# The expert stage of a mixture-of-experts encoder layer in 32-token blocks: plain f32 products on 32-column tiles, three experts' weights on chip

## What is computed

```python
e_idx, gw = route(uf, w_router, router_bias)   # best of 8 groups, then best 2 of its 4 experts
...
def expert_block(args):                        # xblk: tokens of one expert
    xblk, e = args
    h = jax.nn.silu(xblk @ w_gate[e]) * (xblk @ w_up[e])   # 1024 -> 512, twice
    return h @ w_down[e]                                   # 512 -> 1024
...
y = segment_sum(yb * buf_w[:, None], buf_tok, num_segments=N)
```

## Time and profile before

| | |
|---|---|
| runs (median, range) | 2013.12 us (2011.57 to 2013.32), 3 runs |
| profiled execution | 2008.88 us, of which the traced span is 2007.0 us |
| expert stage in the trace | 1233.7 us (first transposes) to 1948.7 us (last write issued) |
| after it | 58.3 us to the end of the span |
| PE busy over the span | 87% |

### The profile page before, as it was taken

The page is one execution under the profiler, slowest core; times in us unless marked ns, Lnnn a source line. Parts: engine busy times, 40 slices in busy tenths (PEclk is TensorE's granted clock), DMA queues, the critical chain, the costliest instruction groups (busy, mean ns, idle before and its releaser), DMA issues.

```text
span 2007.0 us, 24786 instructions
## 1 busy us (share of the span) xinstructions
PE 1742.4 (87%) x8132; PEld 1397.1 (70%) x8133; DVE 1128.1 (56%) x1313; ACT 863.5 (43%) x1011; POOL 457.7 (23%) x303
## 2 busy tenths in 40 slices
PE   3899999999776999999989923999999999999970
PEld 1767787776545787787868822877777777777760
DVE  1534343445766334343236671466888878878538
ACT  1423333334653111101022120467887887878623
POOL 3411122211123333233312123111221212212112
PEclk7989999999887999999999956999999999999995
DMA  8101111101502333341222143476999999999626
GB/s 287 42 22 42 31 41 31 41 11 28 195 0 84 112 113 100 99 152 47 89 95 97 42 180 106 188 303 261 380 393 376 382 387 375 388 384 376 280 101 234
DMA packets 124566, 346.03 MB, mean 172 GB/s; under 512 B 17758, under 2 KB 79846, under 8 KB 112238
## 3 DMA queue, kind: packets, MB, share of 16 engines
q1 hardware_dynamic: 99678, 272.55, 36.4%
q0 software_dynamic: 10800, 36.77, 5.3%
q10 hardware_dynamic: 14048, 36.20, 5.1%
HBM read 309.21 MB, written 36.29 MB: 172 GB/s over the span
## 4 chain that ended last, share of the span: by engine, by line
PE 67%; DVE 14%; DMA 6%; ACT 4%; issue 2%; POOL 1%; ACTq 0%; DVEq 0%; POOLq 0%; SPq 0%
PE ps L678 22%; PE ps L904 8%; PE ps L905 7%; PE ps L909 7%; PE ps L838 5%; PE ps L863 4%; DMA raw_u<-in_w_exp_up 3%; PE ps L754 3%; PE ps L720 3%; DMA ada_g<-in_ada_w 1%; PE ps L745 1%; PE ps L804 1%; DVE wg_lo L354 1%; DVE wu_lo L354 1%; DMA raw_g<-in_w_exp_gate 1%
## 5 line engine op out<-in xcount | busy, mean ns | idle before, releaser
L678 PE MATMUL ps<-u_hi,w_hi 128*128 128x512 f32 x768 | 315.2, 410 | 16.9 <-POOL w_lo L514 16.3
L678 PE MATMUL ps<-u_hi,w_lo 128*128 128x512 f32 x768 | 302.9, 394 | 0.0
L678 PE MATMUL ps<-u_lo,w_hi 128*128 128x512 f32 x768 | 302.7, 394 | 0.0
L678 PEld LDWEIGHTS ps<-u_hi,w_hi 128*128 128x128 f32 x768 | 146.3, 190 | 50.2 <-issue 24.4
L513 POOL CAST w_hi<-w_raw 128x1024 fp32r<-128x1024 f32 x48 | 53.0, 1104 | 538.5 <-PE ps L678 453.7
L678 PEld LDWEIGHTS ps<-u_hi,w_lo 128*128 128x128 f32 x768 | 145.6, 190 | 31.9
L678 PEld LDWEIGHTS ps<-u_lo,w_hi 128*128 128x128 f32 x768 | 146.7, 191 | 25.7
L354 DVE TENSOR_TENSOR wd_lo<-raw_d,wd_hi 128x2048 fp32r<-128x2048 f32 x64 | 143.8, 2288 | 23.7 <-ACT wd_hi L350 23.7
L616 POOL COPY tok_cur<-tokl 128x1 int32 x37 | 26.8, 723 | 545.4 <-PE ps L893 545.4
L1088 ACT ACTIVATE gate<-ps,bg 128x512 f32<-128x512 f32 x48 | 33.0, 689 | 270.3 <-PE ps L678 229.4
L354 DVE TENSOR_TENSOR wu_lo<-raw_u,wu_hi 128x2048 fp32r<-128x2048 f32 x64 | 143.4, 2280 | 0.0
(11 more groups left out here) (277 smaller groups left out, 3598.0 us busy)
## 6 DMA issues: line engine op xcount, KB each, us to landing
raw_g<-in_w_exp_gate SPq DMA_DIRECT2D x32, 2048.0 KB, 9.4
raw_u<-in_w_exp_up SPq DMA_DIRECT2D x32, 2048.0 KB, 10.4
raw_d<-in_w_exp_down SPq DMA_DIRECT2D x32, 2048.0 KB
d_y<-yb ACTq DMA_DIRECT2D x37, 512.0 KB, 9.7
ada_g<-in_ada_w ACTq DMA_DIRECT2D x32, 512.0 KB, 3.8
w_raw<-in_w_in SPq DMA_DIRECT2D x24, 512.0 KB, 4.1
w_raw<-in_w_branch_gate SPq DMA_DIRECT2D x24, 512.0 KB, 4.1
ada<-in_ada_w SPq DMA_DIRECT2D x4, 2048.0 KB, 15.1
```

The source lines that it names most:

```text
L678: ins = pe.matmul(ps[:, 5 + h, :], a[par][:, kc, :], b[:, kc, HF[h]], start=(n == 1), stop=(n == MM))
```

## The change

The expert stage is rewritten. Blocks have 32 tokens. A block's 32 rows of 1024 are gathered as 128 pieces of 1 KB, so that all 128 partitions are used. The products are plain f32, without a split: gate and up together are 8 steps of four matmuls (32 stationary columns, 256 moving columns, one for each quarter of the output), down is 4 steps of four. The raw weights are used as they land, in three slots (`w_exp`, 48 KB per partition each); slot reuse waits for the last block of the expert three back (`gu_ps`, `y_ps`). Experts come in the order 0, 4, 8, ..., 28, 1, 5, ..., since `group_at` is the identity. ACT, DVE and POOL have one loop over all blocks; PE's experts are unrolled. In each turn PE transposes the hidden rows of block j-1 and the gathered rows of block j+1, does gate and up of block j, and down of block j-1 (numbered from 1; the first turn's down is of nothing, so there are 94 writes).

```diff
-CAP = 128
-NBLK = 2048 // CAP + NE
+CAP = 32
+LEAST = 2
+NBLK = 2048 // CAP + LEAST * NE
+SLOTS = 3
+QT = D // 4
...
+def group_at(g):
+    return g
+def expert_at(i):
+    return EPG * group_at(i % NG) + i // NG
...
+            for i in range(SLOTS, NE):
+                used = sp.value_load(starts[0:1, i - 2:i - 1], min_val=LEAST + 1, max_val=NBLK + 1)
+                sp.wait_ge(gu_ps, used)
+                for w in "gu":
+                    load_expert(i, w)
+                sp.wait_ge(y_ps, used)
+                load_expert(i, "d")
...
-                pool.wait_ge(xg_ps, j + 1)
+            with pool.Fori(1, end) as j:
+                pool.wait_ge(ld_xg, j * 16)
                 hold(pool)
                 pool.tensor_copy(tok_cur[:], tokl[:, bass.ds(j + 1, 1)]).then_inc(tok_ready, 1)
-                pool.wait_ge(tok_ready, j + 2)
+                pool.wait_ge(tok_ready, j + 1)
+                pool.wait_ge(xg_ps, j)
                 hold(pool)
+                gather_rows()
...
+            def gate_up(sl):
+                for kc in range(KC):
+                    x = xT[:, kc % 2, CAP * (kc // 2):CAP * (kc // 2 + 1)]
+                    for n in range(4):
+                        off = part_of["gu"[n // 2]] + kc * FE + QT * (n % 2)
+                        last = pe.matmul(ps[CAP * n:CAP * (n + 1), 2, 0:QT], x, w_exp[:, sl, off:off + QT],
+                                         start=(kc == 0), stop=(kc == KC - 1))
+                last.then_inc(gu_ps, 1)
...
+            def turn(j, sl, d_slot):
+                hidden_turn(j)
+                pe.wait_ge(xT_ready, j)
+                pe.wait_ge(ld_xg, j * 16 + 16)
+                hold(pe)
+                rows_to_features()
+                gate_up(sl)
+                down_turn(j, d_slot)
...
             def output(j):
-                sc.wait_ge(y_ps, j + 1)
-                sc.wait_ge(st_y, j * 16 + 16)
-                sc.activation(yb[:], ps[:, 5:7, :].rearrange("p a b -> p (a b)"), ACT.Copy).then_inc(y_evac, 1)
+                sc.wait_ge(y_ps, j)
+                sc.wait_ge(st_y, j * 16)
+                sc.activation(yb[:], ps[:, 4, 0:QT], ACT.Copy).then_inc(y_evac, 1)
...
-                sc.dma_start(d_y[bass.ds(j * CAP, CAP), :], yb[:]).then_inc(st_y, 16)
+                sc.dma_start(d_y[bass.ds(j * CAP - CAP, CAP), :].rearrange("t (n m) -> n t m", n=4), yb[:]).then_inc(st_y, 16)
...
+            with sc.Fori(1, end) as j:
+                sc.wait_ge(gu_ps, j + 1)
+                sc.activation(act[2 * CAP:P, :], ps[0:2 * CAP, 2, 0:QT], ACT.Silu).then_inc(silu_ready, 1)
+                output(j)
```

More of the change, by code:

```diff
@@ L241, in build @@
         tok = small("tok", [P, TT], i32)
-        tokl = small("tokl", [P, LIST], i32)
+        quarter = small("quarter", [P, 1], i32)
+        quarter_f = small("quarter_f", [P, 1])
         pair_w = small("pair_w", [P, 2, TT])
@@ L346, in half_of @@
             return a[:, half * n:(half + 1) * n, :]
[L348 to L354, removed]
         def hold(eng):
@@ new lines, in _ @@
+            for t in range(TT):
+                if t == TT - 1:
+                    sp.wait_ge(mo_ps, 2 * TT)
+                    sp.dma_start(before[:], k_before).then_inc(ld_rt, 16)
+                    for g in range(NG):
+                        src = router_bias[EPG * group_at(g):EPG * group_at(g) + EPG].partition_broadcast(P)
+                        sp.dma_start(rbias[:, EPG * g:EPG * (g + 1)], src).then_inc(ld_rt, 16)
+                    for w in "gud":
+                        load_expert(0, w)
@@ L471, in _ @@
-            load_weights(1)
-            sp.wait_ge(st_list, 16 * 2 * TT)
[L473 to L478, removed]
+                load_expert(1, w)
+            sp.wait_ge(st_u2, 16 * TT)
+            sp.wait_ge(x2t_ps, TT)
+            for w in "gud":
+                load_expert(2, w)
@@ L479, in _ @@
+            sp.wait_ge(st_list, 16 * 2 * TT)
+            for q in range(4):
+                sp.dma_start(tokl[CAP * q:CAP * (q + 1), :], d_list.rearrange("(p l) o -> p (l o)", p=CAP)).then_inc(ld_list, 16)
+            sp.wait_ge(slots_ready, 1)
             sp.dma_start(gffn[:], d_mod[3].partition_broadcast(P)).then_inc(ld_end, 16)
@@ new lines, in hidden_to_features @@
+            def hidden_to_features():
+                for c in range(2):
+                    last = pe.transpose(ps[:, 3, c * 2 * CAP:(c + 1) * 2 * CAP], act[2 * CAP:P, c * P:(c + 1) * P], ident[2 * CAP:P, 2 * CAP:P])
+                last.then_inc(ht_ps, 1)
+            def gate_up(sl):
[6 more added lines that the diff above has]
+                last.then_inc(gu_ps, 1)
@@ new lines, in down, with hidden_turn @@
+            def down(slot):
+                for fc in range(FC):
+                    h = actT[:, fc % 2, CAP * (fc // 2):CAP * (fc // 2 + 1)]
+                    for n in range(4):
+                        off = part_of["d"] + fc * D + QT * n
+                        last = pe.matmul(ps[CAP * n:CAP * (n + 1), 4, 0:QT], h, w_exp[:, slot, off:off + QT], start=(fc == 0), stop=(fc == FC - 1))
+                last.then_inc(y_ps, 1)
+            def hidden_turn(j):
+                pe.wait_ge(act_ready, j)
+                hold(pe)
+                hidden_to_features()
@@ new lines, in _ @@
+            rows_to_features()
[3 more added lines that the diff above has]
+                pe.wait_ge(ld_xg, j * 16 + 16)
+                hold(pe)
+                rows_to_features()
+                gate_up(sl)
+                down_turn(j, d_slot)
+            for i in range(NE):
+                sl, loads = slot_at(i), 16 * (i // SLOTS + 1)
+                first = pe.value_load(starts[0:1, i:i + 1], min_val=1, max_val=NBLK)
+                end = pe.value_load(starts[0:1, i + 1:i + 2], min_val=LEAST + 1, max_val=NBLK + 1)
+                for w in "gu":
+                    pe.wait_ge(ld_wt[w][sl], loads)
+                if i == 0:
+                    pe.wait_ge(ld_wt["d"][sl], loads)
+                turn(first, sl, slot_at(max(i - 1, 0)))
+                if i:
+                    pe.wait_ge(ld_wt["d"][sl], loads)
+                with pe.Fori(first + 1, end) as j:
+                    turn(j, sl, sl)
@@ L937, in _ @@
+            hidden_turn(end)
+            down_turn(end, slot_at(NE - 1))
         @block.scalar
@@ L1151, in output @@
+                sc.wait_ge(st_y, j * 16)
+                sc.activation(yb[:], ps[:, 4, 0:QT], ACT.Copy).then_inc(y_evac, 1)
+                sc.wait_ge(y_evac, j + 1)
                 hold(sc)
-                sc.dma_start(d_y[bass.ds(j * CAP, CAP), :], yb[:]).then_inc(st_y, 16)
-            def next_hi(w, e, used, end):
-                sc.wait_ge(used, end)
-                sc.wait_ge(ld_raw[w], e * 16 + 32)
-                hold(sc)
-                for half in range(2):
-                    split_hi(w, half)
@@ L1623, in _ @@
+            hidden_features(end)
             dve.wait_ge(ld_end, 16 * 3)
```

276 lines of the change are left out of this document (92 added, 184 removed).

## The result

The changed kernel takes **2052.78 us** (median of 4 runs, 2051.0 to 2055.99) against 2013.21 us for the kernel before: a ratio of 1.020, 95% interval 1.018 to 1.022. The forecast was 2058 us, in a range of 1925 to 2120. The profiled execution spans 2054.2 us.

What follows compares the result with a forecast made beforehand. The one-buffer write of `yb` on four engines was taken to bound turns while weights load: 57.7 at 9.3 us, 35.3 at 6.4, 763 us. With 1231, 3 and 58.3 us around it, the forecast was 2058 us, range 1925 to 2120.

Steps and rivals of the forecast that it cites:

- the likeliest case: Expert stage: write of `yb` confined to four DMA engines, with one buffer; 2005 to 2100 us, chance 0.57.
- PE's turn, 6.4 us: Expert stage, only PE counting: 48 products 5.5 us, four transposes 0.60, waits 0.3; 595 us for 93 turns.
- the rival of 0.45 us a product: PE's tiles don't run side by side at full clock: 21.7 us a turn, stage 2020 us; chance 0.01.
- The weights: Expert loads: 6.29 MB take 15.3 us at 410 GB/s; three experts can be on chip when the stage begins.
- Four engines: Write of `yb`: its outermost count of 4 makes it use 4 DMA engines, each moving 32 KB of a block.
- The landing, 7.7 to 9.7 us: Write of `yb` beside weights: 2.6 us undisturbed plus contention; with copy and signals a loaded turn takes 9.3 us.
- A full landing in every loaded turn: Expert stage: during 537 us of loads 57.7 turns take 9.3 us; the other 35.3 take 6.4 us.
- Ahead of and behind the stage: Stage begins at 1231 us, first turn at half clock adds 3 us, last stage keeps 58.3 us.
- PE's unrolled code, costed at nothing: Expert stage: its fetches were expected behind the 1.8 us of a down product; a microsecond per expert would be 32 us.
- The clock: Rival: PE's clock falls in every loaded turn, a turn 12 us, 2141 us in all; chance 0.09.
- The first rival, sixteen engines: Write of `yb` is not confined; the gather becomes the longest wait, 1946 us, or 1889 if it hides; chance 0.30.
- the 6.6 that I took beside weights: Gather into `xg` in the first rival's case: 6.6 us beside weights, 7.2 with transposes and waits.

Runs made afterwards that it cites:

- run 10: Run 8 with each write of `yb` cut into four of 32 rows, on sixteen engines, every row in its place: 1861.77 us.
- run 1: The changed kernel with the write of `yb` over an outermost count of 128 instead of 4, rows misplaced: 1968.66 us.
- run 8: Run 5 with the expert groups in the order of the kernel before (0, 2, 7, 3, 1, 4, 6, 5): 1917.04 us.
- run 3: The changed kernel with two buffers `yb`, the write still on four engines: 1973.64 us.
- run 5: Run 3 with two buffers `xg` as well and PE's turns written out for the 93 blocks: 1943.48 us.
- run 9: Run 8 with the write of `yb` over an outermost count of 128, rows misplaced as in run 1: 1860.71 us.
- run 7: The changed kernel with no weights loaded after the third expert, so another result: 1867.72 us.

## Why the prediction was right

It named the likeliest case, the write of `yb` on four engines with one buffer, and that case came. Step by step:

- **PE's turn, 6.4 us: 6.0.** 48 products take 5.32 us (the chain puts 3.59 us on gate and up and 1.73 on down), 0.111 each for the 0.114 that came from the 32 records of the earlier trace rows. The rest was too dear: four transposes take 0.7 us, and there are no waits of 0.3 us besides. Four tiles side by side is right; the rival of 0.45 us a product is refuted in every row.
- **The weights.** 15.3 us an expert was right: the loaded stretches run at 352 to 358 GB/s on average with holes in them, run 10 at 409. Three experts were on chip in time.
- **Four engines.** ACT's queue shows it:

```profile
q10 hardware_dynamic: 21128, 29.12, 4.5%
```

  21128 packets are 94 x 128 rows of `d_y`, 32 x 256 runs, 8 rows, and 896 over; 32 x 16 and 8 x 1 of those belong to the other transfers, and 376 = 94 x 4 are left. Run 1 has 22256 packets, 94 x 12 more: sixteen for each write. Both counts agree with the rule of the Trainium skill (DMA: Bandwidth & Descriptors, section "Why a DMA increments its semaphore by 16 and not by 1"), which is here measured at 4 and at 16.
- **The landing, 7.7 to 9.7 us: too low.** 29 landings take 10.7 to 12.2 us (11.39 above), a turn that they set 12.0 us and not 9.3 (347 us in 29). This is the one term outside its bounds, and the packets of ACT's queue in the trace say which part of it. With no weights beside it a write has its first packet 1.2 us after the issue starts, its rows take 1.7 us, and 0.35 us later the last report is in: 3.3 us, for the 2.6 that I had carried over from the write on sixteen engines. In the 29 the rows take 6.9 us. That is 5.2 more, 0.16 for each of an engine's 32 packets, and the turns with 4 KB packets that I had at 5.1 are right. But the first packet goes only after 4.0 us, 2.8 more, where I had a fixed 1.7. So 3.3 + 5.2 + 2.8 = 11.3 us stand for my 2.6 + 5.1 + 1.7 = 9.4. Why the first packet waits 2.8 us longer beside weights is open.
- **A full landing in every loaded turn: no.** The loaded time was right: weights are on the way for 544 us of the stage (packets of SP's queue, gaps of over 0.5 us left out), for 537. With turns of 12.0 us for 537 us and 6.0 us for the rest the sum would have said 537 / 12.0 = 44.8 turns and 48.2 x 6.0, 827 us. Measured are 755.8 for the forecast's 763, because a load does not hold every turn to a full landing: a write that goes out as a load ends finds free engines (issued at 1287.8 us, it landed in 5.8). In the 544 us fall some 55 turns, 9.9 us each, for 57.7 at 9.3; the other 38 take 212 us, 5.6 each, for 35.3 at 6.4. They are under 6.0 us where PE's products stood ready behind a late copy. The even picture of two turns of about 9 us per two-block expert did not come: turns beside weights swing between 3.9 and 12.8 us. So the agreement of 2052.8 with 2058 rests on two misses of opposite sign, a full landing longer than I had it and fewer turns that pay it. That they cancel is luck.
- **Ahead of and behind the stage.** The first transposes of the stage stand at 1225 us and its first products at 1230.2, for a stage that begins at 1231, the first turn at half clock costs 2.7 us for 3, and 59.4 us follow the last write for 58.3. PE's unrolled code, costed at nothing, shows no stop of size: all waits that the trace puts on nothing come to 6 us on the transposes. The sum ended at 2057 us for a run like the profiled one; with the 4 us by which that run lay below the median it is 2061, not 2058.
- **The clock.** In the loaded stretches it was 0.88 and 0.90, not 0.50, with PE idle for a quarter of them. That rival, a fall in every loaded turn, is refuted. Falls there are: 22 stretches of the stage, 99 of its 756 us, stand at 0.50. This one costs nothing:

```profile
1318.00:1324.00 6.00, 5.07 (x44) 2.18 (x40) 0.72 (x2) 0.92 (x2) 0.98 (x1) 0.50 1.03 416
```

  From 1318 to 1324 us PE is at half clock, and its 5.47 us of gate and up end before the write of `yb`, issued at 1316.4, lands at 1327.5. Where PE was the bound a fall did cost: 2.6 us behind the stop of run 8. What the 22 cost together no run tells. The Trainium skill's warning (TensorE: Matmul & The Clock Gate, section "HAM oscillation — how this bites in real kernels") is borne out in part: the clock came down again and again, but 22 times beside 32 turns of over 10 us, and not each time.
- **The first rival, sixteen engines**, was priced at 1946 us and measured in run 1 at 1968.7; its mechanism, the gather as the next wait, was right. Landings of the gather are 2.7, 6.0 and 7.3 us (least, median, most) in the changed kernel, for the 6.6 that I took beside weights, POOL's 1.0 included:

```profile
DMA to landing us min/median/max: 2.7/6.0/7.3
```

The question behind it all, where the gain of a cheaper PE turn went: 93 turns of 6.0 us are 558 us, 157 less than the 715 of before. The kernel before waited for its writes in the shadow of an 18.9 us block; in a 6.0 us turn the shadow is gone. The waits of one `yb`, one `xg` and the four engines ate 198 us, and runs 3, 5, 8 and 10 give 191 of them back: 79 for the second `yb`, 30 for the second `xg` (with PE's turns written out), 26 for the order, 55 for the sixteen engines.

What stays open is why a write's first packet waits so long beside weights, and what PE's written-out turns are worth alone.

## What to carry to other kernels

When a change makes a loop's turn three times shorter, list every wait that recurs once per turn with its landing under load, not its landing alone, and put each beside the new turn: what exceeds it needs a second buffer before the shorter turn is worth anything. Waits of this kind stand in line behind each other, so an edit that measures nothing alone (the order, the second `xg`) can be worth 26 or 30 us behind the others: test them on top of the cure of the first, too. And look at the outermost count of each transfer: a small write on four of sixteen engines delays itself, and, as runs 8 and 9 show, the large loads that share those engines too.

## What the runs showed of the hardware that was not expected

- A write of 128 rows of 1 KB on four engines lands in 10.7 to 12.2 us where 4 KB weight packets flow beside it throughout (the changed kernel), and in 3.3 us without them (there and in run 7). On sixteen it takes some 7 us and 1.7 (runs 1 and 9, medians), and with two buffers it is never waited for (run 9).
- The confined write still costs 56 us with two buffers (runs 8 and 9, nothing but its spread changed). Its landing in run 8 is 12.7 us in the median beside weights, more than two turns of 6.0, and ACT still waited 242 us for it. By a count of the turns that is most of the cost: 65 turns of 6.4 to 8.5 us lie 52 us above 6.0 each, and the three longest 23 us above, where the two longest of run 9 lie 12 above.
- Late engines show in a load's reports: with the confined write and two buffers, in 50 of 62 loads twelve reports come within 3.3 us and the last four some 14 us later (median, run 8); with all sixteen engines for the write no load has this (runs 9 and 10).
- An issue on ACT of the write over four engines takes 554 ns, over sixteen 338, and a part of 32 rows 321:

```profile
L1180 ACTq DMA_DIRECT2D d_y<-yb x94: 554/555/1202, 1239.0 to 1994.8; - x94
```

```profile
L1180 ACTq DMA_DIRECT2D d_y<-yb x94: 338/338/379, 1238.6 to 1911.7; - x94
```

The first row is the changed kernel's, the second that of run 1 (least, median and most ns).
